# Decay columns first, and four norm weights multiplied into the weights behind them, in a two-layer hybrid trunk on one core

## The chip, the cores and the metric

One Trainium2 chip, one core. The metric is the device time of one execution in microseconds (us). Everything is float32. Products that must be accurate are split by hand into a rounded high part and a rest: three matmuls (high x high, high x rest, rest x high) give one product.

## The reference, cut to what matters

The input x has 256 tokens of 1024 channels. Two layers:

```
def rms_norm(x, w):
    y = x * lax.rsqrt(mean(x * x, -1) + EPS)
    return y * w
hn = rms_norm(h, attn_norm_w[0]);  proj = hn @ w_in            # q, k, v, gate, 16 tail columns
qkv = silu(causal_conv(proj[..., :3072]))
beta = sigmoid(b_logit);  g = -exp(a_log) * softplus(a_logit + dt_bias)   # the tail columns
h = h + (gated delta rule, gated norm) @ w_out
h = h + swiglu(rms_norm(h, ffn_norm_w[0]))                     # d_ff 2816
kv = rms_norm(h, kv_norm_w) @ w_kv                             # shared K and V
q  = rms_norm(h, attn_norm_w[1]) @ w_q;  h = h + attention(q, kv) @ w_o
hn = rms_norm(h, ffn_norm_w[1]);  logits = hn @ router_w
h = h + (top 2 of 8 SwiGLU experts of hn, d_ff 3584)
return rms_norm(h, final_norm_w)
```

## The kernel before, in words

Each engine has its own written-out program, and they meet on semaphores. PE is the matrix engine, DVE the vector engine, ACT the scalar engine, POOL GpSimd, SP the engine that only issues loads. The order on each engine is the order of the code.

**Norms.** A norm k (0 to 5: attention 0, dense, K/V, attention 1, experts, final) is done in two halves of 128 tokens. ACT squares and sums (`square`, L609), POOL makes the reciprocal root (`norm_rstd`, L532 and L533), DVE multiplies by it and by the norm's weight row, which lies broadcast over all partitions (`norm_x`, L945), PE turns the result to channel-major (`turn`, L1478), and ACT and DVE copy it out of the accumulator banks (`turned`, L628 and L955). K/V and queries have the same h and the same reciprocal root, but other weight rows: norms 2 and 3 are two multiplications and two rounds of transposes of the same h.

**Start.** PE turns norm 0, computes the 16 tail columns for half of the tokens (`tail_columns`, L1495, 32 small matmuls in 64 records), transposes the convolution weights (L1504), and goes to `qkv(0)`: first the lower half of the contraction for four column tiles, then the other two groups of tail columns, then the upper half. DVE copies the convolution weights (L961), makes the rest of x (L973) and then the rests of the weights (`q_rest`, L967); ACT makes their high parts (`q_round`, L637); POOL makes every second rest (L540). The tail columns go through ACT exp, DVE (L1000 to L1005), ACT exp and ln, and behind these on ACT stands the first convolution tap (`first_tap`, L676). Each of the 24 column tiles then takes a first tap on ACT, three taps on DVE (`convolve`, L987) and a SiLU on ACT (L662).

**K, V and queries.** After the last down product of the dense MLP, DVE adds to h (L1160), norm 2 follows, and for each token half PE turns x and computes K (L1845) and V (L1851). Then come a swap of halves (L1855), `turn(3)` for the second norm, and the queries (L1869).

**Router and experts.** After attention PE merges heads through w_o (L1928) in 512-column halves, turns norm 4, computes the router's logits (L1968) and counts (L1973 to L1980). DVE takes the two best (`top_two`, L1323 to L1329), makes positions and one-hot matrices (L1341 to L1354), then the rest of the first up weights (`w_rest`, L1169), then the rest of the gathered x (`gathered`, L1383). PE gathers tokens by matmul (L1987) and starts the first expert (`e_proj`, L1508 to L1510). ACT makes the high part of those up weights (`w_round`, L758) after an exp that waits for DVE. Behind `gathered` DVE has the list of items (L1424 to L1444) and then the rest of the next gate weights. The eight experts are blocks of seven steps; a step loads gate, up and down weights of 2 MB each, and SP issues each load as soon as the rest of the slot's former tile is made.

Of the kernel before, what the change touches and what calls it, by code (L numbers as in the profile page):

```python
# [23 lines left out]
P = 128  # L24
# [101 lines left out]
def trunk(nc, ins, consts, cat, out):  # L126
    ctx = ExitStack()
    with ctx:
# [140 lines left out]
        cw = view(sm, 24, CONV * 24)  # L269
        alog = view(sm, 120, 8)  # L270
# [72 lines left out]
        s_oss, s_orstd = sem("s_oss"), sem("s_orstd")  # L343
# [28 lines left out]
        NATIVE = {0: 0, 2: 1, 3: 2, 4: 3}  # L372
# [28 lines left out]
        def _(sp):  # L401
# [57 lines left out]
            for t in range(NT):  # L459
                sp.wait_ge(s_xn, 4 * 4 + 2 * t + 2)  # L460
                sp.dma_start(xn_rows[t * P:(t + 1) * P, :], xn[:, t, :]).then_inc(s_rows, 16)
# [42 lines left out]
            for t in range(NT):  # L504
                for q in range(2):
                    sp.wait_ge(s_xn, 4 * 5 + 2 * t + q + 1)
# [6 lines left out]
        def _(pool):  # L513
# [5 lines left out]
            pool.dma_start(relb[0:BUCKETS, :], ins["rel_bias"]).then_inc(s_relb, 16)  # L519

# [72 lines left out]
        def _(act):  # L593
            link = Chain(act, ach)
            names = [ins["attn_norm_w"][0:1, :], ins["ffn_norm_w"][0:1, :], None,
                     ins["attn_norm_w"][1:2, :], ins["ffn_norm_w"][1:2, :], None]
            names[2] = ins["kv_norm_w"].rearrange("(a n) -> a n", a=1)
            names[5] = ins["final_norm_w"].rearrange("(a n) -> a n", a=1)

            def row_load(k):  # L600
                if k >= 2:
                    act.wait_ge(s_xn, 4 * (k - 2) + 4)
# [14 lines left out]
            def turned(k, groups=range(4)):  # L617
                if k not in NATIVE:
                    for g in groups:
                        t, q = divmod(g, 2)  # L620
                        act.wait_ge(s_tp, 4 * k + g + 1)
# [4 lines left out]
                for g in (g for g in groups if g % 2 == 0):  # L626
                    act.wait_ge(s_tp, 4 * k + g + 1)
# [54 lines left out]
            act.wait_ge(s_small, 16 * 4)  # L682
# [8 lines left out]
            act.activation(nx, nx, ACT.Ln, bias=K("one")).then_inc(s_soft, 1)  # L691
            act.wait_ge(s_cw, 1)
# [77 lines left out]
            row_load(2)  # L770
            row_load(3)
# [50 lines left out]
            for t in range(NT):  # L822
                squares(2, s_h, 4, [t])
                turned(2, [2 * t])
# [11 lines left out]
            turned(3)  # L836
            row_load(4)
            row_load(5)
# [96 lines left out]
        def _(dve):  # L935
            link = Chain(dve, vch)

            def norm_x(k, t):
                if t == 0:
                    dve.wait_ge(s_row[k % 2], 16 * (k // 2 + 1))  # L940
                r = rstd_of(k)
                dve.wait_ge(s_rstd, 2 * r + t + 1)
                for q in range(2):
# [8 lines left out]
            def turned(k, tiles=range(NT)):  # L952
                for g in (2 * t + 1 for t in tiles):
                    dve.wait_ge(s_tp, 4 * k + g + 1)
# [5 lines left out]
            dve.wait_ge(s_cwt, 1)  # L960
# [191 lines left out]
            for n in range(2, NC):  # L1152
                gate_out(n)
# [981 lines left out]
```

## Time and profile before

| | us |
|---|---|
| median of 3 runs | 1515.43 (1514.69 to 1516.58) |
| the profiled execution, its own time | 1515.32 |
| its span, first to last instruction | 1513.5 |
| PE busy | 1472.8 (97% of the span) |
| DVE busy | 1121.9 (74%) |
| ACT busy | 895.3 (59%) |

A busy share says little here by itself: the profile is read by stage. Times in the trace count from the span's start. A row with x64 joins that many records; a matmul's duration overlaps that of the next, so the pace is read from starts or from a group's whole length.

### The profile page before, as it was taken

The numbers are of one execution on the slowest core, as the hardware profiler recorded it, in microseconds if no ns is written. First come the engines' busy times: TensorE is split into PE (matmuls) and PEld (weight loads), VectorE is DVE, ScalarE is ACT, GpSimd is POOL, SyncE is SP. The second block draws the span as 40 slices with busy tenths as digits, with TensorE's granted clock in tenths as the row PEclk, the third lists the DMA queues.
The fourth block names the chain that finished last, engine by engine and source line by source line (L and its number), as shares of the span: only waits on it lengthen the run. The fifth ranks groups of instructions, "written<-read, shape, count | busy, mean of one in ns | idle before, by whom it ended". The sixth has DMA issues, their size and how long they took to land.

```text
span 1513.5 us, 22634 instructions
## 1 busy us (share of the span) xinstructions
PE 1472.8 (97%) x8983; PEld 1233.5 (81%) x8983; DVE 1121.9 (74%) x1057; ACT 895.3 (59%) x851; POOL 96.7 (6%) x65
## 2 busy tenths in 40 slices
PE   6999999999989989999999999999999999999998
PEld 6998958999977577888888888888888888888886
DVE  4766355455434388899888898888888998888796
ACT  4540234434324356777777777677776777777674
POOL 4330010000000000001000000000000000000000
PEclk9999999999999989999999999999999999999999
DMA  7541127555543169999999999999999999999993
GB/s 257 183 152 57 43 72 223 188 170 191 206 182 112 59 244 368 394 386 381 395 376 363 388 375 371 389 377 367 379 373 363 397 393 371 393 377 366 380 393 120
DMA packets 194334, 437.97 MB, mean 289 GB/s; under 512 B 5280, under 2 KB 28096, under 8 KB 194160
## 3 DMA queue, kind: packets, MB, share of 16 engines
q1 hardware_dynamic: 189248, 423.64, 76.0%
q0 software_dynamic: 2736, 9.24, 2.4%
q10 hardware_dynamic: 2304, 4.43, 0.8%
q8 instruction: 35, 0.57, 0.2%
q14 instruction: 11, 0.09, 0.0%
HBM read 429.41 MB, written 7.88 MB: 289 GB/s over the span
## 4 chain that ended last, share of the span: by engine, by line
PE 86%; DVE 7%; ACT 4%; DMA 2%; issue 1%; POOL 1%; DVEq 0%; SPq 0%; ACTq 0%; POOLq 0%
PE bank L1508 23%; PE bank L1510 23%; PE bank L1509 23%; PE bank L1869 2%; PE bank L1928 2%; PE bank L1737 2%; DVE ws L987 2%; PE bank L2043 2%; PE bank L1547 1%; DVE weights_lo L1169 1%; ACT qkv_hi L637 1%; DMA weights<-in_moe_w_down 1%; DMA weights<-in_moe_w_up 1%; PE bank L1652 1%; PE bank L1635 1%
## 5 line engine op out<-in xcount | busy, mean ns | idle before, releaser
L1169 DVE TENSOR_TENSOR weights_lo<-weights,weights_hi 128x2048 fp32r<-128x2048 f32 (+1 forms) x396 | 823.4, 2121 | 142.2 <-ACT weights_hi L758 140.4
L758 ACT ACTIVATE weights_hi<-weights 128x2048 fp32r<-128x2048 f32 (+1 forms) x396 | 685.5, 1782 | 258.8 <-DMA weights<-in_moe_w_up 92.4
L1508 PE MATMUL bank<-weights_hi,expert_x_hi 128*128 128x512 f32 x896 | 354.9, 396 | 1.4 <-DVE expert_x_lo L1383 1.1
L1510 PE MATMUL bank<-weights_hi,expert_x_lo 128*128 128x512 f32 x896 | 349.4, 390 | 0.0
L1509 PE MATMUL bank<-weights_lo,expert_x_hi 128*128 128x512 f32 x896 | 349.2, 390 | 0.0
L1508 PE MATMUL bank<-weights_hi,hidden_hi 128*128 128x512 f32 x520 | 204.4, 393 | 1.5 <-DVE hidden_lo L1207 1.5
L1509 PE MATMUL bank<-weights_lo,hidden_hi 128*128 128x512 f32 x520 | 202.6, 390 | 0.0
L1510 PE MATMUL bank<-weights_hi,hidden_lo 128*128 128x512 f32 x520 | 202.5, 389 | 0.0
L1510 PEld LDWEIGHTS bank<-weights_hi,expert_x_lo 128*128 128x128 f32 x896 | 168.3, 188 | 36.4
L1508 PEld LDWEIGHTS bank<-weights_hi,expert_x_hi 128*128 128x128 f32 x896 | 168.2, 188 | 35.4 <-DVE expert_x_lo L1383 1.2
L1509 PEld LDWEIGHTS bank<-weights_lo,expert_x_hi 128*128 128x128 f32 x896 | 168.4, 188 | 33.4
L1508 PEld LDWEIGHTS bank<-weights_hi,hidden_hi 128*128 128x128 f32 x520 | 97.7, 188 | 22.2 <-DVE weights_lo L1169 2.3
L1510 PEld LDWEIGHTS bank<-weights_hi,hidden_lo 128*128 128x128 f32 x520 | 97.6, 188 | 20.6
L1509 PEld LDWEIGHTS bank<-weights_lo,hidden_hi 128*128 128x128 f32 x520 | 97.7, 188 | 19.4
L1508 PE MATMUL bank<-x_hi,weights_hi 128*128 128x256 f32 x320 | 90.9, 284 | 1.2 <-issue 1.2
L1510 PE MATMUL bank<-x_hi,weights_lo 128*128 128x256 f32 x320 | 90.5, 283 | 0.0
L1509 PE MATMUL bank<-x_lo,weights_hi 128*128 128x256 f32 x320 | 90.5, 283 | 0.0
L777 ACT ACTIVATE ws<-bank 128x512 f32<-128x512 f32 x67 | 39.6, 592 | 82.0 <-PE bank L1510 81.7
L1508 PEld LDWEIGHTS bank<-x_hi,weights_hi 128*128 128x128 f32 x320 | 61.4, 192 | 1.8 <-issue 1.4
L1509 PEld LDWEIGHTS bank<-x_lo,weights_hi 128*128 128x128 f32 x320 | 61.4, 192 | 0.4
L1510 PEld LDWEIGHTS bank<-x_hi,weights_lo 128*128 128x128 f32 x320 | 61.4, 192 | 0.0
L1508 PE MATMUL bank<-qkv_x_hi,qkv_hi 128*128 128x256 f32 x192 | 56.1, 292 | 4.8 <-DVE qkv_x_lo L973 3.7
(312 smaller groups left out, 1498.9 us busy)
## 6 DMA issues: line engine op xcount, KB each, us to landing
weights<-in_moe_w_down SPq DMA_DIRECT2D x56, 2048.0 KB, 9.8
weights<-in_moe_w_up SPq DMA_DIRECT2D x56, 2048.0 KB, 9.7
weights<-in_moe_w_gate SPq DMA_DIRECT2D x55, 2048.0 KB, 9.5
weights<-in_a_w_in SPq DMA_DIRECT2D x7, 2048.0 KB, 8.9
weights<-in_ffn_w_up SPq DMA_DIRECT2D x11, 1024.0 KB, 5.3
weights<-in_ffn_w_gate SPq DMA_DIRECT2D x11, 1024.0 KB, 5.4
weights<-in_ffn_w_down SPq DMA_DIRECT2D x11, 1024.0 KB, 5.0
weights<-in_a_w_out SPq DMA_DIRECT2D x2, 2048.0 KB, 8.1
```

The costliest lines, as they stand in the source:

```text
L637: act.activation(qhi[(c + 1) % 2][:, w_], slot[c % 3][:, w_], ACT.Copy).then_inc(q_hi, 1)
L758: act.activation(hi[:, j * n:(j + 1) * n], slot[k][:, j * n:(j + 1) * n], ACT.Copy).then_inc(w_hi[k], 1)
L777: act.activation(act_h, bank[0][:, :], ACT.Silu).then_inc(m.act, 1)
L987: i_ = dve.scalar_tensor_tensor(out=dst[:, sh:T], in0=src[:, 0:T - sh], scalar=cw[:, w:w + 1], in1=dst[:, sh:T], op0=ALU.mult, op1=ALU.add)
L1169: dve.tensor_tensor(to[:, c], slot[k][:, c], hi[:, c].bitcast(F32), ALU.subtract).then_inc(w_lo[k], 1)
L1508: pe.matmul(dst, ah, bh, start=start, stop=False, skip_group_check=True)
L1509: pe.matmul(dst, ah, bl, start=False, stop=False, skip_group_check=True)
L1510: return pe.matmul(dst, al, bh, start=False, stop=stop, skip_group_check=True)
L1737: m = pe.matmul(bank[banks[q]][:, :], xt[:, kt, t * P:(t + 1) * P], g8[slots[q]][:, kt, :], start=kt == 0, stop=kt == KT - 1)
L1869: m = pe.matmul(bank[3 + g % 2][:, j * T:(j + 1) * T], g8[k][:, kt, c], xt[:, kt, :], start=kt == 0, stop=kt == KT - 1)
L1928: m = pe.matmul(bank[2 * t + q][:, :], oT[:, kt, t * P:(t + 1) * P], g8[q][:, kt, :], start=first and kt == kts[0], stop=last and kt == kt ...
L2043: m = pe.transpose(bank[2][:, j * P:(j + 1) * P], hid[:, j * P:(j + 1) * P], ident)
```

## The change

It does four things. All large buffers keep their addresses: the new small columns lie in gaps.

1. At the start, all four groups of tail columns are computed before `qkv(0)`; the transposes of the convolution weights now also turn three norm-weight vectors (24 more rows, loaded by three small DMAs on POOL's queue). ACT does the exp and ln of the tail ahead of the high parts of the second weight tile; DVE makes the rest of x first and copies the convolution weights after the first weight rest.
2. K/V and queries: DVE multiplies h by the reciprocal root only. ACT multiplies w_kv, and both halves of w_q, in place by the weight column of their norm (`fold`: eight instructions of 128x512 each). Norm 3 with its multiplications, transposes and copies is gone, and so are two row loads. The transposes of the second token half move between K and V of the first.
3. Router: DVE multiplies the router's matrix by the norm weight ahead of time. PE turns h itself instead of norm 4; DVE scales the logits by the reciprocal root. Norm 4's own multiplication, which the gather and the rows in memory still need, comes after.
4. The last merge is cut in two with the first logits between; the first expert's first product waits for each half of the gathered x by itself.

```diff
 ACT, start
             act.wait_ge(s_small, 16 * 7)
             act.activation(alog, alog, ACT.Exp).then_inc(s_soft, 1)
-            for j in range(2):
-                q_round(1, j)
             act.wait_ge(s_tail, 1)
...
             act.activation(nx, nx, ACT.Ln, bias=K("one")).then_inc(s_soft, 1)
+            for j in range(2):
+                q_round(1, j)
             act.wait_ge(s_cw, 1)
 ACT, dense MLP's first norm
-            row_load(2)
-            row_load(3)
+            row_load(4)
+            row_load(5)
 ACT, after the last hidden tile
-            for t in range(NT):
-                squares(2, s_h, 4, [t])
-                turned(2, [2 * t])
+            def fold(i):
+                act.wait_ge(loaded[i], 16 * (PRE_A[i] + 1))
+                for kt in range(KT):
+                    a = act.activation(g8[i][:, kt, :], g8[i][:, kt, :], ACT.Copy, scale=wcol[min(i, 1)][:, kt:kt + 1])
+                a.then_inc(s_fold, 1)
+
+            act.wait_ge(s_cw, 1)
+            fold(0)
+            squares(2, s_h, 4, [0])
+            turned(2, [0])
+            squares(2, s_h, 4, [1])
+            fold(1)
+            turned(2, [2])
+            fold(2)
             act.wait_ge(s_kmm, 1)
...
-            turned(3)
-            row_load(4)
-            row_load(5)
 DVE
+                if k == 2:
+                    for q in range(2):
+                        c = slice(q * 512, (q + 1) * 512)
+                        dve.tensor_scalar(xn[:, t, c], h[:, t, c], rs[:, r, t:t + 1], None, ALU.mult).then_inc(s_xn, 1)
+                    return
...
-            dve.wait_ge(s_cwt, 1)
-            dve.tensor_copy(cw, bank[7][:, 0:96]).then_inc(s_cw, 1)
-            dve.wait_ge(s_cw, 1)
...
             q_rest(0, 1)
-            q_rest(1, 0)
+            dve.wait_ge(s_cwt, 1)
+            for i in range(3):
+                dve.tensor_copy(wcol[i], bank[7][:, 96 + KT * i:96 + KT * i + KT])
+            dve.tensor_copy(cw, bank[7][:, 0:96]).then_inc(s_cw, 1)
+            dve.wait_ge(s_cw, 1)
             def convolve(n):
-                if n % 4 == 0 and 0 < n < 20:
+                if n % 4 == 0 and n < 20:
                     q_rest(n // 4 + 1, 0)
...
+            dve.wait_ge(s_router, 16)
+            dve.tensor_tensor(router[:, :, :], router[:, :, :], wide(wcol[2], E), ALU.mult).then_inc(s_cw, 1)
...
-            dve.wait_ge(s_tp, 12)
-            norm_xn(3)
...
-            turned(3)
 DVE, top_two and its caller
-                link(dve.tensor_copy(logit[:, t, :], bank[4][:, t * 8:t * 8 + 8]))
+                dve.wait_ge(s_rstd, 2 * rstd_of(4) + t + 1)
+                link(dve.tensor_scalar(logit[:, t, :], bank[4][:, t * 8:t * 8 + 8], rs[:, rstd_of(4), t:t + 1], None,
+                                       ALU.mult))
...
-            for t in range(NT):
-                add_h(t, s_aw, 0, (0, 1, 2, 3), 8)
-                norm_x(4, t)
-                if t:
-                    top_two(0)
-                turned(4, [t])
+            add_h(0, s_aw, 0, (0, 1, 2, 3), 8)
+            turned(4, [0])
+            norm_x(4, 0)
+            add_half(1, 0, s_aw, 0, (0, 1, 2, 3))
+            top_two(0)
+            add_half(1, 1, s_aw, 0, (0, 1, 2, 3))
+            turned(4, [1])
             top_two(1)
+            norm_x(4, 1)
 PE
             ready(0)
+            tail_columns(2)
+            tail_columns(3).then_inc(s_tail, 1)
             pe.wait_ge(s_cwin, 16)
-            pe.transpose(bank[7][:, 0:96], convrow[0:96, :], ident[0:96, 0:96]).then_inc(s_cwt, 1)
+            pe.wait_ge(s_small, 16 * 7)
+            pe.transpose(bank[7][:, 0:120], convrow[0:120, :], ident[0:120, 0:120]).then_inc(s_cwt, 1)
...
-                        if half == 0:
-                            tail_columns(2)
-                            tail_columns(3).then_inc(s_tail, 1)
...
+            turn(2, [0])
             for t in range(NT):
-                turn(2, [t])
...
-                pe.wait_ge(loaded[0], 16 * (PRE_A[0] + 1))
+                pe.wait_ge(s_fold, 1)
...
+                else:
+                    turn(2, [1])
...
-            turn(3)
-            ready(3)
...
             turn(4, [0])
-            merge(1, range(8), [1])
-            pe.wait_ge(s_router, 16)
+            merge(1, range(4), [1])
+            pe.wait_ge(s_cw, 2)
             for t in range(NT):
                 if t:
+                    merge(1, range(4, 8), [1])
                     turn(4, [1])
...
             def first_gather():
+                pe.wait_ge(s_xn, 4 * 3 + 4)
...
-            pe.wait_ge(m_Xl, 2)
-            e_proj(0, 0, m_g)
+            e_proj(0, 0, m_g, rows=m_Xl)
```

## Rows read from the trace of the kernel before

**Rows 1.** The page, part 4: the chain that ended last, by engine.
```profile
PE 86%; DVE 7%; ACT 4%; DMA 2%; issue 1%; POOL 1%; DVEq 0%; SPq 0%; ACTq 0%; POOLq 0%
```
**Rows 2.** Windows, expert stage: length, busy of PE, PEld, DVE, ACT, POOL; clock, DMA.
```profile
1090.00:1190.00 100.00, 100.00 (x459) 82.80 (x459) 88.67 (x57) 73.23 (x51) 2.79 (x1) 1.00 1.02 374
```
**Rows 3.** Timeline of the start: start, length, engine, work, idle before and its releaser.
```profile
13.67 3.59 PE L1495 MATMUL bank<-ws,xt 128*64 128x8 f32 x64
14.45 4.55 POOL L540 TENSOR_TENSOR qkv_lo<-weights,qkv_hi 128x2048 fp32r<-128x2048 f32 x1 [3.99 <-ACT qkv_hi L650]
...
17.65 0.26 DVE L961 COPY sm<-bank 128x96 f32<-128x96 f32 x1 [3.18 <-PE bank L1504]
17.94 3.27 DVE L973 TENSOR_TENSOR qkv_x_lo<-xt,qkv_x_hi 128x1024 fp32r<-128x1024 f32 x2
...
21.14 2.28 DVE L967 TENSOR_TENSOR qkv_lo<-weights,qkv_hi 128x2048 fp32r<-128x2048 f32 x1
21.27 0.58 PE L1508 MATMUL bank<-qkv_x_hi,qkv_hi 128*128 128x256 f32 x1 [3.66 <-DVE qkv_x_lo L973]
...
23.95 3.73 ACT L637 ACTIVATE qkv_hi<-weights 128x2048 fp32r<-128x2048 f32 x2 [5.30 <-DMA weights<-in_a_w_in]
...
28.81 2.04 PE L1495 MATMUL bank<-ws,xt 128*64 128x8 f32 x64
...
31.52 1.14 DVE L1002 SCALAR_TENSOR_TENSOR sm<-sm 128x16 f32<-128x16 f32 x1
...
34.44 0.46 ACT L676 ACTIVATE ws<-bank,sm 128x256 f32<-128x256 f32 x1
```
**Rows 4.** The two instructions of line L973: shortest, median, longest in ns.
```profile
L973 DVE TENSOR_TENSOR qkv_x_lo<-xt,qkv_x_hi x2: 1214/1676/2137, 17.9 to 20.0; 128x1024 fp32r<-128x1024 f32 x2
```
**Rows 5.** Windows of PE alone, at the start: length, busy, matmuls, clock, DMA.
```profile
33.00:35.00 2.00, 2.00 (x19) 1.00 0.00 0
```
**Rows 6.** Timeline of the K, V and query stage.
```profile
416.43 0.63 ACT L609 ACTIVATE ws<-h 128x512 f32<-128x512 f32 x1 [7.50 <-DVE h L1160]
...
418.96 1.41 DVE L945 SCALAR_TENSOR_TENSOR xn<-h,sm,norm_row 128x512 f32<-128x512 f32 x2 [1.97 <-POOL sm L533]
...
421.60 0.69 DVE L955 COPY xt<-bank 128x512 f32<-128x512 f32 x1
...
422.40 3.81 PE L1845 MATMUL bank<-xt,weights 128*128 128x128 f32 x32 [1.31 <-issue]
...
431.52 3.81 PE L1845 MATMUL bank<-xt,weights 128*128 128x128 f32 x32 [0.98 <-DVE xt L955]
...
439.48 1.04 PE L1478 MATMUL bank<-cst,xn 128*128 128x128 f32 x8
...
443.39 14.05 PE L1869 MATMUL bank<-xt,weights 128*128 128x256 f32 x64 [0.83 <-ACT xt L628]
```
**Rows 7.** Loads issued at 399.98 and 400.49: size, and us from issue to landing.
```profile
weights<-in_w_kv SPq DMA_DIRECT2D x1, 2048.0 KB, 10.5
weights<-in_b_w_q SPq DMA_DIRECT2D x1, 2048.0 KB, 15.4
```
**Rows 8.** Timeline from the router's logits to the first expert.
```profile
527.89 1.11 PE L1968 MATMUL bank<-router,xt 128*64 128x8 f32 x32
...
534.24 1.88 PE L1968 MATMUL bank<-router,xt 128*64 128x8 f32 x32 [0.88 <-DVE xt L955]
...
539.81 5.79 PE L1987 MATMUL bank<-ws,xn 128*128 128x128 f32 x32 [0.57 <-DVE ws L1345]
...
541.04 4.49 DVE L1169 TENSOR_TENSOR weights_lo<-weights,weights_hi 128x2048 fp32r<-128x2048 f32 x2
...
547.02 0.50 PE L1508 MATMUL bank<-weights_hi,expert_x_hi 128*128 128x512 f32 x1 [1.07 <-DVE expert_x_lo L1383]
...
558.53 0.50 PE L1508 MATMUL bank<-weights_hi,expert_x_hi 128*128 128x512 f32 x1 [0.32 <-DVE weights_lo L1169]
```
**Rows 9.** Load issued at 528: the first expert's first up weights.
```profile
weights<-in_moe_w_up SPq DMA_DIRECT2D x1, 2048.0 KB, 8.4
```

More of the change, by code:

```diff
@@ L269, in trunk @@
         cw = view(sm, 24, CONV * 24)
+        wcol = [view(sm, 372, KT), view(sm, 380, KT), view(ws, 28296, KT)]
         alog = view(sm, 120, 8)
@@ L519, in _ @@
             pool.dma_start(relb[0:BUCKETS, :], ins["rel_bias"]).then_inc(s_relb, 16)
+            for i, w in enumerate((ins["kv_norm_w"], ins["attn_norm_w"][1], ins["ffn_norm_w"][1])):
+                pool.dma_start(convrow[96 + KT * i:96 + KT * i + KT, :],
+                               w.rearrange("(k p) -> k p", p=P)).then_inc(s_small, 16)
             def rstd(dst, src, n, sem_out, inv):
@@ L594, in _ @@
             link = Chain(act, ach)
[L595 to L598, printed above, removed]
+            names = {0: ins["attn_norm_w"][0:1, :], 1: ins["ffn_norm_w"][0:1, :], 4: ins["ffn_norm_w"][1:2, :],
+                     5: ins["final_norm_w"].rearrange("(a n) -> a n", a=1)}
             def row_load(k):
-                if k >= 2:
-                    act.wait_ge(s_xn, 4 * (k - 2) + 4)
+                if k >= 4:
+                    act.wait_ge(s_xn, 4 * (k - 4) + 4)
                 act.dma_start(rows[k % 2][:, :], names[k].to_broadcast([P, D])).then_inc(s_row[k % 2], 16)
@@ L938, in norm_x @@
             def norm_x(k, t):
-                if t == 0:
-                    dve.wait_ge(s_row[k % 2], 16 * (k // 2 + 1))
                 r = rstd_of(k)
+                if t == 0 and k != 2:
+                    dve.wait_ge(s_row[k % 2], 16 * (k // 4 + 1))
                 dve.wait_ge(s_rstd, 2 * r + t + 1)
+                if k == 2:
[3 more added lines that the diff above has]
+                    return
                 for q in range(2):
@@ L995, in _ @@
             dve.wait_ge(s_bexp, 1)
-            dve.wait_ge(s_small, 16 * 4)
+            dve.wait_ge(s_small, 16 * 7)
             tail = view(bank[5], 0, NC, 8)
@@ L1470, in turn @@
                     for q in range(2):
-                        pe.wait_ge(s_xn, 4 * k + 2 * t + q + 1)
+                        if k == 4:
+                            pe.wait_ge(s_h, 8 + 2 * t + q + 1)
+                        else:
+                            pe.wait_ge(s_xn, 4 * k + 2 * t + q + 1)
                         if t and k in NATIVE:
@@ L1477, in turn @@
                             kt = 4 * q + j
-                            m = pe.transpose(bank[6 + q][:, j * P:(j + 1) * P], xn[:, t, kt * P:(kt + 1) * P], ident)
+                            m = pe.transpose(bank[6 + q][:, j * P:(j + 1) * P],
+                                             (h if k == 4 else xn)[:, t, kt * P:(kt + 1) * P], ident)
                         m.then_inc(s_tp, 1)
@@ L1848, in _ @@
                     m.then_inc(s_kmm, 1)
+                else:
+                    turn(2, [1])
                 vm = bank[(5, 2)[t]]
@@ L1862, in query @@
                 if g % 2 == 0:
-                    pe.wait_ge(loaded[k], 16 * (PRE_A[k] + 1))
+                    pe.wait_ge(s_fold, k + 1)
                 if g >= 2:
@@ L2027, in _, with e_proj @@
             eh, el = view(xeh, 0, KT, P), view(xel, 0, KT, P)
-            def e_proj(k, s, done, free=None):
+            def e_proj(k, s, done, free=None, rows=None):
                 if free is not None:
@@ L2033, in e_proj @@
                 for kt in range(KT):
+                    if kt % 4 == 0 and rows is not None:
+                        pe.wait_ge(rows, kt // 4 + 1)
                     if kt % 4 == 0:
```

24 lines of the change are left out of this document (13 added, 11 removed).

## The prediction

> **What bounds the kernel now.** I read the page first. The chain that ended last is matrix work for 86% of the span, DVE for 7% and ACT for 4% [rows 1], so most of the time lies where this change touches nothing. The windows over the expert stage say the same: PE is busy for the whole 100 us at clock 1.00, and the DMA engines are busy throughout too, at 374 GB/s [rows 2]. Nothing there gets shorter; it can only begin earlier. What the change can move are three places where PE isn't the bound: the start, the K/V and query stage, and the way from the router to the first expert. For each I read the timeline engine by engine and asked which instruction starts last.
>
> *Start.* PE stands still between its first tail columns (end 17.26) and 21.27, when DVE has made the rest of x. The lower half of `qkv(0)` then takes until 28.81, the other tail columns 2.0, and from 34.44 on the first taps run [rows 3]. From here ACT and DVE alternate, tap by tap, for all 24 column tiles, and PE waits for them, so the stage is a queue that starts at the first tap: whatever brings that tap forward brings all 24 forward. The tap isn't late because of PE; it stands on ACT behind exp and ln of the tail, and these behind DVE's L1002, which ends at 32.66.
>
> *K, V, queries.* From 422.40 PE works almost without a gap, but a part of it is the second turn of the same h: transposes from 439.48, and queries only at 443.39 [rows 6].
>
> *Router.* PE waits again and again from 529.0, the end of the first logits. Its first expert product at 547.02 is released by DVE's rest of x, behind which DVE's item list runs; the next gate product at 558.53 again waits for DVE [rows 8].
>
> **The change, part one: the start.** The second two groups of tail columns follow the first directly, 17.26 + 3.6 (the same 64 records as at 13.67) = 20.9; the transposes take about 0.4 (the copy behind them starts at 17.65), so PE is free at 21.2 to 21.3. DVE could begin the rest of x earlier now, since the copy is no longer ahead. But the first of the two instructions took 2137 ns and the second 1214 [rows 4]: the first began at 17.94, and POOL's subtraction ran until 19.00 [rows 3]. The 0.92 us more are nearly the 1.06 of overlap, so I let DVE stand still behind POOL here. Started at 15.9 it would be released at 19.0 all the same and be done at 21.3. So `qkv(0)` starts at 21.3 as before. Its lower half still takes 7.5, to 28.8, but the upper half follows at once. Its first tile is twelve matmuls, at 19 in 2.00 us [rows 5] 1.3, at the mean pace of the lower half (48 in 7.5) 1.9: ready at 30.1 to 30.7.
>
> The other input of the tap is ACT. DVE ends the first weight rest at 23.4, copies four small pieces (0.26 for the large one, so 0.3 to 1.0 together), and adds the bias (the whole way from the end of the tail columns, 30.85, to L1002 was 0.7, of which a part was ACT's). L1002 itself took 1.14 for 16 columns, which I can't price: 0.2 if it also stood behind POOL, 1.14 if not; I take 0.3, as POOL has nothing to do then. That gives 24.6 (upper bound 26.2). From L1002's end to the tap were 1.8, and the two high parts of the second tile, which now stand in between, cost 3.73 [rows 3]: 30.1. The first tap starts at 30.4 instead of 34.44: **4.0 us less**, between 2.6 and 4.3. What was hidden before and isn't now: those 3.7 us of ACT; they lie beside PE's lower half, and only if the small chain is late do they show. POOL's next rest starts after them, ends at about 35, and is wanted by PE at 35.8. Three more DMAs on POOL's queue, before its first arithmetic, land while everything still waits for x. What is queued behind PE's new wait for them is `qkv(0)`, which has until 21.2.
>
> **Part two: K, V and queries.** The folds are 24 instructions of 128x512 on ACT. The nearest row is the squaring, 0.63 each [rows 6], so 5.0 per fold. Fold 0 stands ahead of the squares, but ACT was idle for 7.5 us before 416.43. The K/V weights land at 400.0 + 10.5 = 410.5 [rows 7], the fold ends at 415.5, the squares start at 416.43 as before: nothing, with 0.9 to spare. Fold 1 (weights there at 415.9) starts after the second squares at about 422 and ends at 427, fold 2 at 432. The copy of x that waits behind fold 1 isn't wanted before the first V is done (about 430); the copies of K wait behind fold 2 until about 434. The last weights are issued at about 410.5, and even with the longer landing, 15.4, they are there before fold 2. So the folds cost nothing; without that cover they would cost 15.
>
> The normalisation has one operand less. Its row is 1.41 for two halves, with a weight row [rows 6]; the trace has no wide multiplication by a column alone. Bounds: 0.75 each as now, and the 0.28 of a quarter-size one as a floor. I take 0.5, so the copy at 421.60 and K behind it come 0.5 earlier, at 421.9. The Trainium skill (VectorE: DVE Perf Modes, the perf-mode tier table) has 1227 ns for such an operation on 2048 float32 elements in SBUF against 2293 with two tensors; by that ratio each half would be an estimated 0.40 and the gain 0.7. No row here shows it.
>
> PE's work from the first K to the second turn was 422.40 to 439.48, 17.1. The 0.98 of waiting for a copy goes, because K of the other half is now behind V: 16.1. Then 421.9 + 16.1 = 438.0, and the queries follow at 438.1 instead of 443.39: **5.2 us less** (4.8 to 5.7). The four multiplications, 16 transposes and four copies of norm 3 are all in that difference. Two row loads less and two issued elsewhere are beside PE's work.
>
> **Part three: the router.** The first logits now stand ahead of the merge's last half, whose end moves from 527.9 to 529.0. After it, the transposes need only one addition (0.7, as the copies) instead of addition, squares, root and multiplication: logits of the second half at 529.0 + 0.7 + 0.5 (four transposes) + 0.1 + 0.7 = 531.0 instead of 534.24, 1.1 us long as the first or 1.9 as the second [rows 8]. `top_two` comes 3.2 to 4.0 earlier. DVE then has the multiplication of norm 4 (1.4) in front of the positions, at least partly beside PE's counts, so the gather starts 1.8 to 4.0 earlier than 539.81. But that isn't the last input. DVE must first make the rest of the up weights, 4.49, and these are loaded when the merge ends: 529.05 + 8.4 = 537.5 [rows 9], 1.1 later than now. The high parts take 1.9 each (half of 3.73), so DVE runs from 539.3 to 543.8, where it ended at 545.5. **1.7 us less** on DVE. PE starts the expert 2.4 earlier, since it needs only half of the rest of x, but at the next gate product it waited for DVE already, so what is kept is DVE's 1.7. Upper bound 2.9 (the weights are no limit), lower 0 (they land as late as the K/V ones, 10.5). In the expert stage each load is issued by a finished rest, so the loads move with it.
>
> **The sum.** 4.0 + 5.2 + 1.7 = 10.9. The profiled execution has 1515.3 (its span 1513.5 and 1.8 around it), so 1504.4; it is 0.1 below the median of the runs, so I predict **1504.5**. The bounds of the terms make 7.4 to 12.9, 1502.5 to 1508.
>
> **Rivals.**
> - *The router's way gives nothing, or the start only its 2.6.* For it: the up load is issued later and shares the engines with six stores; ACT's chain at the start has three links that I bounded only. Against: later stores leave it more room. 1506.
> - *More.* The load lands early, the multiplication is fast: 4.1 + 5.6 + 2.9 give 1502.8.
> - *Two of the three don't come,* only the queries' part does, with a little: 1509.
> - *A fold shows.* If the K/V weights land 3 us later, the squares start 2 us late and all behind them: 1506.5.
> - *Slower: the expert stage becomes bound by its loads.* DMA is busy for all of it [rows 2], and a step's 6.3 MB at 374 GB/s take just its 16.8 us. If the new phase between PE and the loads stretched a step by more than 10.9 / 56 = 0.19 us, the gain would be gone; at 0.3 the time is 1521. Against: PE has no gap at all, and SP issues on DVE's progress, which shifts as a whole.
> - *No change at all* would need the three waits to be refilled; I see nothing that could do it.
>
> **How the numbers follow.** Forecast 0.46, more 0.19, less at 1506 (with the fold) 0.24, 1509 0.05, slower 0.04, none 0.02. A measurement here tells 0.2%, 3 us, from no change: faster 0.94, same 0.02, slower 0.04. The range 1500.8 to 1508.3 takes in the forecast and its neighbours on both sides and leaves out the last three.
>
> **What would show it.** Right: first L676 near 30.4 and L1508 still near 21.3; queries starting 9.2 earlier than before, 5.2 of it since the dense stage; the squares at the same distance from the last down product; the gate product after the first expert's two 10.9 earlier; 16.8 us per step. Wrong: ACT's fold row directly before the squares with the squares late; the up weights' high part waiting for a DMA beyond 8.4; PE gaps in the expert stage.

## The result and the profile after

The changed kernel takes **1504.42 us** (median of 5 runs, 1502.97 to 1507.0) beside 1515.43 for the kernel before on the same chip (median of 5, 1514.39 to 1520.91). The ratio is 0.9922, with a 95% interval of 0.9909 to 0.9934. Predicted were 1504.5, in a range of 1500.8 to 1508.3. A second set of 5 runs gave 1503.76 and 0.992 [0.9903, 0.9936]. The profiled execution has a span of 1503.0 us against 1513.5, so 10.5 less.

The page of the changed kernel, parts 1 and 4: busy time with its share of the span, and the chain that ended last.

```profile
PE 1467.2 (98%) x8967; PEld 1229.4 (82%) x8967; DVE 1117.8 (74%) x1055; ACT 907.9 (60%) x873; POOL 100.0 (7%) x68
...
PE 78%; DMA 7%; DVE 7%; ACT 5%; issue 3%; POOL 1%; DVEq 0%; SPq 0%; ACTq 0%
```

ACT has 12.6 us more work in a shorter kernel: the folds are 15 us, and its two copies for norm 3, 0.6 us each, are gone. The chain stays matrix work in the main [rows 1]. DMA's part of it is 7% here and was 2% before, but a second trace of the same changed kernel has 1%, so this share differs from one execution to the next.

**The start.** Timeline of the changed kernel; it answers to [rows 3].

```profile
13.37 4.83 PE L1520 MATMUL bank<-ws,xt 128*64 128x8 f32 x128
...
14.45 4.58 POOL L544 TENSOR_TENSOR qkv_lo<-weights,qkv_hi 128x2048 fp32r<-128x2048 f32 x1 [3.83 <-ACT qkv_hi L652]
...
15.83 5.41 DVE L984 TENSOR_TENSOR qkv_x_lo<-xt,qkv_x_hi 128x1024 fp32r<-128x1024 f32 x2 [1.66 <-ACT qkv_x_hi L657]
...
21.17 2.28 DVE L978 TENSOR_TENSOR qkv_lo<-weights,qkv_hi 128x2048 fp32r<-128x2048 f32 x1
21.30 0.58 PE L1536 MATMUL bank<-qkv_x_hi,qkv_hi 128*128 128x256 f32 x1 [2.71 <-DVE qkv_x_lo L984]
...
24.28 0.17 DVE L1017 SCALAR_TENSOR_TENSOR sm<-sm 128x16 f32<-128x16 f32 x1
...
24.49 0.22 ACT L690 ACTIVATE sm<-sm 128x16 f32<-128x16 f32 x1 [5.77 <-DVE sm L1017]
...
26.23 3.71 ACT L639 ACTIVATE qkv_hi<-weights 128x2048 fp32r<-128x2048 f32 x2
...
30.95 0.47 ACT L678 ACTIVATE ws<-bank,sm 128x256 f32<-128x256 f32 x1 [1.01 <-PE bank L1538]
```

The rest of x (L984 here) starts on DVE 2.1 us earlier, and yet `qkv(0)` begins at 21.30, as before (21.27). The small chain is short: L1017 takes 0.17 us where it took 1.14. ACT is ready for the first tap at 29.94. The tap starts at 30.95, because it waits 1.01 us for PE. Before, it started at 34.44, so the start gives 3.5 us.

**K, V and queries.** Timeline of the changed kernel; it answers to [rows 6].

```profile
407.03 5.02 ACT L827 ACTIVATE weights<-weights,sm 128x512 f32<-128x512 f32 x8 [1.64 <-DMA weights<-in_w_kv]
...
412.16 1.29 DVE L1175 TENSOR_TENSOR h<-h,bank 128x512 f32<-128x512 f32 x2 [4.57 <-PE bank L1538]
...
412.88 0.63 ACT L611 ACTIVATE ws<-h 128x512 f32<-128x512 f32 x1 [0.83 <-DVE h L1175]
...
415.39 0.88 DVE L956 TENSOR_SCALAR xn<-h,sm 128x512 f32<-128x512 f32 x2 [1.94 <-POOL sm L537]
...
418.29 3.81 PE L1870 MATMUL bank<-xt,weights 128*128 128x128 f32 x32 [1.27 <-issue]
418.34 5.00 ACT L827 ACTIVATE weights<-weights,sm 128x512 f32<-128x512 f32 x8
...
423.72 4.99 ACT L827 ACTIVATE weights<-weights,sm 128x512 f32<-128x512 f32 x8
...
434.15 2.10 PE L1894 MATMUL bank<-xt,weights 128*128 128x256 f32 x9
```

The first fold ends at 412.05 (407.03 + 5.02) and the squares start at 412.88, released by DVE's addition to h, not by the fold. The other two folds lie beside K and V. The queries start at 434.15 instead of 443.39. That is 9.24 less, of which 3.55 came with the start (the addition to h at 412.16 instead of 415.71).

**From the router to the first expert.** Timeline of the changed kernel; it answers to [rows 8].

```profile
515.14 1.11 PE L1994 MATMUL bank<-router,xt 128*64 128x8 f32 x32
...
519.91 0.37 SPq L408 DMA_DIRECT2D weights<-in_moe_w_up  x1
...
522.19 1.10 PE L1994 MATMUL bank<-router,xt 128*64 128x8 f32 x32 [0.88 <-DVE xt L970]
...
527.24 5.83 PE L2014 MATMUL bank<-ws,xn 128*128 128x128 f32 x32 [0.76 <-DVE ws L1366]
...
528.67 3.71 ACT L760 ACTIVATE weights_hi<-weights 128x2048 fp32r<-128x2048 f32 x2 [2.06 <-DMA weights<-in_moe_w_up]
530.61 4.49 DVE L1189 TENSOR_TENSOR weights_lo<-weights,weights_hi 128x2048 fp32r<-128x2048 f32 x2 [2.05 <-ACT weights_hi L760]
...
535.76 0.50 PE L1536 MATMUL bank<-weights_hi,expert_x_hi 128*128 128x512 f32 x1 [2.35 <-DVE expert_x_lo L1404]
```

The second logits start 12.05 us earlier and the gather 12.57, but the first expert product only 11.26. The gate product after it, at 547.87, is 10.66 earlier than before and waits 0.92 us for DVE. Between them stands a load: ACT waits 2.06 us for the up weights, DVE 2.05 for ACT, PE 2.35 for DVE.

### The profile page after: what moved, and what is told of

Same layout as the page of the kernel before. It is cut to its first block, busy times and chain, and to the rows that moved or that the text cites. A ratio compares the mean times of both kernels' runs of the same rounds, so it can differ in the third digit from the quotient of the medians.

```text
span 1503.0 us, 22624 instructions
## 1 busy us (share of the span) xinstructions
PE 1467.2 (98%) x8967; PEld 1229.4 (82%) x8967; DVE 1117.8 (74%) x1055; ACT 907.9 (60%) x873; POOL 100.0 (7%) x68
## 4 chain that ended last, share of the span: by engine, by line
PE 78%; DMA 7%; DVE 7%; ACT 5%; issue 3%; POOL 1%; DVEq 0%; SPq 0%; ACTq 0%
PE bank L1536 21%; PE bank L1538 21%; PE bank L1537 21%; DMA weights<-in_moe_w_gate 6%; PE bank L1953 2%; PE bank L1894 2%; PE bank L1762 2%; DVE weights_lo L1189 2%; DVE ws L1002 2%; PE bank L1572 1%; PE bank L2072 1%; ACT weights_hi L760 1%; ACT qkv_hi L639 1%; PE bank L1677 1%; DMA weights<-in_moe_w_up 1%
## 5 line engine op out<-in xcount | busy, mean ns | idle before, releaser
L587 POOL DMA_INDIRECT h_rows<-ws,slot_row x7 | 22.5, 3213 | 574.1 <-DVE ws L1424 490.8
```

Of the source, the lines that this page charges most:

```text
L587: pool.indirect_dma_start(out=h_rows[:, :], out_offset=bass.IndirectOffsetOnAxis(ap=slot_row[1][:, 0:1], axis=0), in_=ye, in_offset=None, ...
```

## The experiments

The traces are compared at three marks: the first tap, the start of the queries, and the first down product of the first expert (at 570.82 before, 560.16 after; from here on most steps take 16.8 us in both, those where the expert changes up to 17.6). All times in us, ratios against the kernel before on the same chip.

| kernel | median (runs) | ratio [95%] | tap | queries | down product | down minus queries |
|---|---|---|---|---|---|---|
| before | 1515.43 | 1 | 34.44 | 443.39 | 570.82 | 127.4 |
| the change | 1504.42 (5) | 0.9922 [0.9909, 0.9934] | 30.95 | 434.15 | 560.16 | 126.0 |
| start only | 1512.30 (11) | 0.9975 [0.9964, 0.9985] | 31.03 | 439.9 | 567.99 | 128.1 |
| all but the start | 1508.14 (6) | 0.9951 [0.9932, 0.9969] | 34.47 | 438.1 | 564.02 | 125.9 |
| all but the router | 1507.67 (5) | 0.9937 [0.9918, 0.9955] | 30.66 | 433.8 | 564.33 | 130.5 |
| folds twice | 1514.04 (10) | 0.9987 [0.9975, 0.9999] | 29.68 | 441.2 | 567.05 | 125.9 |
| logits after the merge | 1502.57 (4) | 0.9904 [0.9889, 0.9919] | 31.26 | 434.5 | 559.13 | 124.7 |
| first rest on DVE | 1505.48 (4) | 0.9920 [0.9905, 0.9935] | 30.61 | 433.9 | 562.57 | 128.7 |
| three moves | 1502.84 (5) | 0.9908 [0.9894, 0.9921] | 29.90 | 433.2 | 557.07 | 123.8 |

### The start alone

Into the kernel before: part 1 of the change, without the three norm-weight vectors.

```diff
+            tail_columns(2)
+            tail_columns(3).then_inc(s_tail, 1)
...
-            for j in range(2):
-                q_round(1, j)
             act.wait_ge(s_tail, 1)
...
+            for j in range(2):
+                q_round(1, j)
```

> The kernel before with the start alone changed (all four groups of tail columns first, exp and ln ahead of the second tile's high parts, rest of x first on DVE); nothing is folded. Theory of separate terms: the first tap starts near 31.0 instead of 34.4 and every later stage keeps its distance to it, so the time is 3.5 us less than before, about 1511.9. Rival, overlap: part of the 3.5 is absorbed by a later wait (w_out's load, the dense stage), and it is under 2 us. If the matrix clock rises at another moment, the tap moves by up to 1.2 us either way.

The tap comes at 31.03, 3.4 earlier, and the queries are 3.5 earlier. By medians it is 3.2 us (1515.52 before in these runs), the ratio 0.9975. So the tap's gain goes through all 24 column tiles undiminished. The down product is 2.8 earlier. Of that stage DVE's rest of the up weights still begins 3.5 earlier (537.56 instead of 541.04), the first expert product only 2.8 (544.19 instead of 547.02); between them the gather takes 6.46 us instead of 5.79, and the second half of DVE's rest of x waits 0.81 for ACT's high part of it.

### All but the start

The change, with the start's order as before.

> The changed kernel with the start as before (only the three weight columns are still turned and copied there). Separate terms: first tap at 34.4 or up to 0.5 later for the three copies, queries 5.7 us earlier than before, first expert's second gate product 7.0 earlier, time about 1508.4. Rival: if the start and the rest overlap, this kernel is as fast as the changed one, 1504 to 1505.

The first tap is where it was (34.47), the queries come 5.2 earlier and the down product 6.8, where 5.7 and, at the gate product before it, 7.0 were expected. The missing 0.5 lies between the first tap and the addition to h, which comes at 416.16, 0.45 later than before; from that addition to the queries the gain is the full 5.7. From the queries to the down product it takes 125.9 us, as in the change. The median is 1508.14, 7.4 less than before.

### All but the router

The change, with norm 4 multiplied ahead of its transposes again, the router's matrix as loaded, and the last merge whole.

```diff
-            merge(1, range(4), [1])
-            pe.wait_ge(s_cw, 2)
+            merge(1, range(8), [1])
+            pe.wait_ge(s_router, 16)
...
-            e_proj(0, 0, m_g, rows=m_Xl)
+            pe.wait_ge(m_Xl, 2)
+            e_proj(0, 0, m_g)
```

> The changed kernel with the router's part undone: norm 4 with its weight before the transposes, the plain router matrix, the merge in one piece, one wait for both halves of the gathered x. Separate terms: the start of the last merge is 9.3 us earlier than before, the second gate product too (549.2), time about 1505.8, 1.3 us over the changed kernel. Rival one: the router's part is worth its full 2.9 (1507.3). Rival two: it is worth nothing, because the first up weights now land later (1504.4).

The median, 1507.67, is 3.3 above the change, more than the router's 1.4. The trace points to a reason: in the attention stage the granted clock fell to 0.50 from 483.0 to 489.8, which the change's trace doesn't have, and which cost some 3.0 us in other pairs of traces (below). Without these, 130.5 would be 127.5, the figure of the kernel before. The five times fall into two groups, 1504.8 to 1505.0 and 1507.7 to 1508.3, as such a drop in some executions and not in others would make them; only one of the five has a trace. So the router's 1.4 rests on the marks, and the medians alone would allow the 2.9 of the first rival.

### Every fold twice

Each of the three folds is done with a plain copy of the same tile ahead of it: the price of the folds when their cover runs out.

```diff
+                for kt in range(KT):
+                    a = act.activation(g8[i][:, kt, :], g8[i][:, kt, :], ACT.Copy)
+                link(a)
                 for kt in range(KT):
                     a = act.activation(g8[i][:, kt, :], g8[i][:, kt, :], ACT.Copy, scale=wcol[min(i, 1)][:, kt:kt + 1])
```

> The changed kernel with each fold preceded by a plain copy of the same tile onto itself, so that a fold takes ACT 10 us instead of 5; what is computed is the same. If the folds are hidden with little to spare ahead of the squares and behind fold 2, the squares start 4.2 late, the copy of x behind fold 1 another 2.6, the copy of K behind fold 2 another 3.4: about 10 us more than the changed kernel, 1514.6. If there were ample cover (the idle time of ACT in the profile is longer than that): within 1 us of 1504.4. If the folds already lay fully on the path: 15 us more, 1519.

Timeline of this kernel, K/V and query stage.

```profile
406.02 4.28 ACT L827 ACTIVATE weights<-weights 128x512 f32<-128x512 f32 x8 [1.45 <-DMA weights<-in_w_kv]
...
410.33 5.01 ACT L830 ACTIVATE weights<-weights,sm 128x512 f32<-128x512 f32 x8
...
411.34 1.28 DVE L1178 TENSOR_TENSOR h<-h,bank 128x512 f32<-128x512 f32 x2 [4.57 <-PE bank L1541]
...
415.25 0.61 ACT L611 ACTIVATE ws<-h 128x512 f32<-128x512 f32 x1
...
418.28 1.09 PE L1505 MATMUL bank<-cst,xn 128*128 128x128 f32 x8 [2.96 <-DVE xn L959]
...
420.64 6.70 PE L1873 MATMUL bank<-xt,weights 128*128 128x128 f32 x32 [1.27 <-issue]
...
440.19 1.12 PE L1885 MATMUL bank<-ws,cst 128*128 128x512 f32 x2 [1.50 <-ACT ws L842]
...
441.15 2.11 PE L1897 MATMUL bank<-xt,weights 128*128 128x256 f32 x9
```

Of 12.8 us of added copies, 7.8 show between the addition to h and the queries (29.8 us instead of 22.0). Three places make it up. The first fold now ends at 415.3, after the addition, so the squares and all behind them are 3.2 late. PE stood still for 2.96 us ahead of the transposes, and then the granted clock fell, to 0.50 in the windows from 420 to 426: the same 32 matmuls take 2.9 more. The copies of K, which stand behind the last fold, hold up the swap by 1.5. So in this trace a fold that is 3 us late costs about 6, with the clock drop that follows the wait. The expectation was 1514.6 and the median is 1514.04, but not by the expected terms: the squares are 3.2 late and not 4.2, the copy of x behind fold 1 shows no wait of PE's, the copy of K 1.5 and not 3.4, and the clock, which had no term, 2.9. The trace is also of the fastest of the ten executions, 1510.3. Its queries are 7.0 us later than the change's, its down product 6.9, where the medians differ by 9.6; what fills the rest in the slower executions isn't shown.

### The logits after the whole merge

PE does the last merge in one piece, and the first logits after it; the second half's logits go to another bank, and DVE takes both halves' two best one after the other. This moves the load of the up weights, which is issued when the merge's last instruction has freed its slot, ahead of 1.1 us of logits.

```diff
-            merge(1, range(4), [1])
+            merge(1, range(8), [1])
             pe.wait_ge(s_cw, 2)
...
                 if t:
-                    merge(1, range(4, 8), [1])
                     turn(4, [1])
```

> The changed kernel with the last merge in one piece again and the first logits behind it (the second half's logits go to another bank), top_two(0) directly ahead of top_two(1). Theory: the router's way is bound by the first up weights, which are loaded when the merge ends; here it ends 1.1 us earlier relative to the merge's start, so the load, ACT's high parts and DVE's rest of these weights all come 1.1 earlier, and the expert's products with them: about 1.1 less than the changed kernel. The logits cost nothing, because they lie beside DVE's addition. Rival: DVE's chain from the logits to the one-hot matrices is the bound; top_two(0) now stands in it, and the time is the same or up to 1 us more. In the trace: ACT's wait for the load of moe_w_up stays in the first case and vanishes in the second.

Timeline of this kernel.

```profile
518.98 0.37 SPq L408 DMA_DIRECT2D weights<-in_moe_w_up  x1
...
527.63 3.71 ACT L760 ACTIVATE weights_hi<-weights 128x2048 fp32r<-128x2048 f32 x2 [1.15 <-DMA weights<-in_moe_w_up]
...
534.73 0.50 PE L1536 MATMUL bank<-weights_hi,expert_x_hi 128*128 128x512 f32 x1 [1.18 <-DVE expert_x_lo L1404]
```

The load is issued 0.93 earlier, ACT's high part, PE's first expert product and the down product all come 1.03 to 1.04 earlier, though this execution's queries were 0.31 later than the change's. Counted from the queries it is 1.3. The logits themselves come later, and that costs nothing: the load is what the expert waits for.

### The first rest on DVE instead of POOL

```diff
-            for c in range(6):
-                pool.wait_ge(q_hi, 2 * c + 2 if c else 1)
+            for c in range(1, 6):
+                pool.wait_ge(q_hi, 2 * c + 2)
...
-            q_rest(0, 1)
+            for half in range(2):
+                q_rest(0, half)
```

> The changed kernel with the very first weight rest made by DVE, behind the rest of x, instead of by POOL beside it. Theory: DVE's rest of x took 5.4 us for two instructions because it stands still while POOL's subtraction of two tensors runs. Without POOL both take 1.2 each, from 15.8 to 18.2, the two weight rests follow until 22.7, qkv(0) can start at 20.5 instead of 21.3, and the small chain is 0.7 earlier: first tap 0.7 to 0.8 earlier than in the changed kernel (30.95), give or take the moment at which the matrix clock rises. Rival: the long duration is the instruction's own (its operands are strided); then the rest of x ends at 21.2 again, the first weight rest at 23.4, and the first tap is 2 us later.

The two instructions of the rest of x, shortest, median and longest in ns, in the change and in this kernel; the first answers to [rows 4].

```profile
L984 DVE TENSOR_TENSOR qkv_x_lo<-xt,qkv_x_hi x2: 1212/2744/4275, 15.8 to 20.0; 128x1024 fp32r<-128x1024 f32 x2
```

```profile
L984 DVE TENSOR_TENSOR qkv_x_lo<-xt,qkv_x_hi x2: 1218/1222/1225, 16.0 to 17.2; 128x1024 fp32r<-128x1024 f32 x2
```

With POOL idle both take 1.22 us, so the length isn't the instruction's own, as the rival had it. With POOL's subtraction beside it the first takes 4.28, and it ends at 20.1, 1.07 us after POOL's end at 19.03: of its 1.22 us it got at most 0.15 done until POOL was through. The Trainium skill (SBUF — State Buffer, two separate sides) describes this as an exclusive lock on a port pair shared by DVE and GpSimd, held for a whole instruction. By that rule the trace agrees. Still the tap is only 0.34 earlier (30.61) and not 0.7 to 0.8, since it waits for PE, 1.30 us here. And PE was no earlier: `qkv(0)` starts at 21.36 and not at the expected 20.5. The rest of x is done at 18.4, but PE is busy with the tail columns until 21.3:

```profile
14.29 7.00 PE L1521 MATMUL bank<-ws,xt 128*64 128x8 f32 x128 [0.66 <-DMA ws<-in_a_w_in]
...
21.36 0.56 PE L1537 MATMUL bank<-qkv_x_hi,qkv_hi 128*128 128x256 f32 x1
```

The same 128 records took 4.83 us in the change; why is told with the prediction's start below. The down product came later than in the change, with 128.7 us behind the queries: this trace too has the clock at 0.78 and 0.53 in the two windows from 480 to 490, and says nothing of the edit there.

### Three moves together

The last two edits, and ten instructions of DVE's item list (count, comparison, running sum) moved from behind `gathered` to the time in which DVE waits for the up weights.

> Both edits before together, and the first ten instructions of DVE's item list (counts, blocks over 128, ranks; 2.0 us) moved ahead of the rest of the first up weights, where DVE stood idle for 2.05 us waiting for the load. Theory: the second gate product waits for DVE's list and rest (0.92 us of PE idle), and the idle time before it can hold a part of the list: 0.7 to 0.8 at the start, 1.1 from the load, 0.9 at the second gate product, together 2.5 to 2.9 less than the changed kernel, 1501.7. Rival: only the part that isn't limited by the load's landing comes, 1 us or less.

Its trace is the shortest of all, a span of 1498.3, with the down product 3.1 earlier than in the change, of which 0.9 is there at the queries. The gate product waits for nothing any more. But its median, 1502.84, is 1.6 below that of the change, with intervals that overlap. So it was timed again, with the change and the merge variant on one chip.

> The change once more, unaltered, to give the two variants a partner that shares their chip and their runs. If the scatter seen so far is what single executions do in the expert stage and in the clock's first rise, the median is 1504.4 within 1.5, the ratio 0.992 within 0.001.

> The change with the whole last merge ahead of the first logits, once more. Theory (the first expert's up weights are issued when the last merge ends, so a shorter way to that point brings the expert forward): 1.1 to 1.3 us less than the unaltered change, about 1503.2. Rival (the 1.9 us seen between medians was scatter, and the load's landing moves with something else): the same as the unaltered change within 0.5.

> The change with three moves, once more. Theory: its trace had the expert's third mark 3.1 us earlier than the change, 2.1 of it behind the start, so 2 to 3 us less than the unaltered change beside it, 1501.5 to 1502.5. Rival (the profiled execution was a lucky one, and only the merge's order counts): as the variant with the merge alone, within 0.5.

| kernel, again | median (runs) | ratio [95%] | queries | down product |
|---|---|---|---|---|
| the change | 1503.76 (5) | 0.992 [0.9903, 0.9936] | 434.25 | 560.05 |
| logits after the merge | 1504.66 (5) | 0.9916 [0.9898, 0.9934] | 434.02 | 561.77 |
| three moves | 1504.16 (6) | 0.9918 [0.99, 0.9936] | 433.12 | 559.98 |

Neither variant is faster than the change by anything that these times can tell, so both expectations of a gain in the median fell; the change itself came within the 1.5 us expected of it. The traces say why a single execution moves by 3 us. Here are windows (length, busy and count of PE, PEld, DVE, ACT, POOL; clock; DMA) of the merge variant's first trace, and of its second, the same kernel.

```profile
480.00:485.00 5.00, 3.84 (x48) 2.51 (x44) 4.46 (x24) 2.36 (x8) 0.00 (x0) 1.00 0.01 3
485.00:490.00 5.00, 5.00 (x30) 2.60 (x29) 2.17 (x7) 3.39 (x17) 0.00 (x0) 1.00 0.00 0
```

```profile
480.00:485.00 5.00, 4.08 (x40) 2.76 (x40) 4.55 (x24) 2.26 (x7) 0.00 (x0) 0.82 0.01 3
485.00:490.00 5.00, 5.00 (x28) 2.82 (x27) 2.48 (x7) 3.11 (x17) 0.00 (x0) 0.50 0.00 0
```

In the second the clock falls to 0.50, its lower level of 1.2 GHz, between 480 and 485 and is back at 490. From the queries to the down product it takes 127.7 us instead of 124.7: 3.1 more. The three-move kernel has 126.9 with the drop and 123.8 without. The change itself has 126.0 and 125.8 in its two traces. So, counted from the queries and without the drop, the merge's order gives 1.1 to 1.3 us and the three moves 2.0 to 2.2, and one drop hides either.

## Why the prediction was right

**The start: mechanism right, 4.0 predicted, 3.5 found.** Right were the order (DVE held by POOL and done at 21.2, `qkv(0)` at 21.30), ACT's chain (ready at 29.94 where 30.1 was predicted), and the small L1017 at 0.17. The tail columns ended at 18.2 (13.37 + 4.83) and not at 20.9, which didn't count, since PE waits for DVE anyway. The reason is the clock. Here are windows (length, busy PE with count; clock; DMA, GB/s) in the change, and in the second trace of the merge variant, whose start is the same:

```profile
14.00:16.00 2.00, 2.00 (x76) 1.00 1.05 387
16.00:18.00 2.00, 2.00 (x44) 0.51 1.06 389
```

```profile
14.00:16.00 2.00, 2.00 (x40) 1.00 1.05 388
16.00:18.00 2.00, 2.00 (x42) 1.00 1.04 384
```

Where the records run at 76 in 2 us, the clock was at its higher level; at 40 to 44 it was at the lower one. (The second trace's clock column can't be used here: its record has no entry before 25.8, and the column shows 1.00 where there is none.) With the lower level throughout, the tail columns take 7.0 us, as twice the 3.6 of the kernel before would have it, and end at 20.9. That is the case in five of the nine other traces with the new start. The mis-sized step is the upper half on PE: the first tile of the upper half was put at 30.1 to 30.7, and the tap waited for PE until 30.95. The lower half's pace was taken from before, 48 matmuls in 7.5 us; in the change the matmuls stood 0.21 us apart until 26.2, in the kernel before until about 25.1, and 0.12 after; the record has the clock's rise from 0.50 to 1.00 at 26.27 in the one and its first entry, 1.00, at 25.12 in the other. In the trace with doubled folds, whose start is the same, this pace ended at 23.9, with the clock's rise, and the tap came at 29.68 with only 0.19 us of waiting for PE. So ACT, ready at 29.94 in the change, would have allowed 4.5, and when the clock rises decides how much of it comes.

**K, V and queries: 5.2 predicted, 5.7 found.** The folds follow one another every 0.62 (predicted 0.63) and cost nothing. The squares wait for h, as predicted, though the margin was 0.83 instead of 0.9. The multiplication by a column alone was sized right: its records are 0.48 to 0.49 long, taken were 0.5, and the pair takes 0.88 instead of 1.41. By the table of the Trainium skill (VectorE: DVE Perf Modes, the perf-mode tier table) the estimate was 0.40; the measured length lies above it. K starts 6.13 after the addition to h where it took 6.69, a gain of 0.56. The prediction's own terms give 438.1 for the queries, 5.3 less and not 5.2. The mis-sized term, and the rest of the difference, is the "16.1": from the first K to the queries it is 15.86 us, and I had 16.1 and 0.1 behind it. The turn between K and V costs 0.87 from its start to V's, where turn and waiting took 2.02 before (429.50 to 431.52), so 1.15 went and not 0.98; and the 0.1 behind the swap isn't there.

**Router: 1.7 predicted, 1.4 found.** The chain went as predicted. Logits and gather came earlier by 2.8 to 3.3 beyond the stages ahead (a part of it by the clock, which was 0.50 at the second logits before and 1.00 in the change: 1.88 and 1.10 us), and the load was what DVE's rest waited for. Counted from the queries it was issued 1.16 later than before (predicted 1.1), and it took 8.7 instead of 8.4: the mis-sized step is the landing. DVE's rest of these weights is therefore done only 1.2 earlier than before, counted from the queries, and not 1.7. Another 0.2 came by something that the prediction had no term for. Before, the second half of DVE's rest of x waited for ACT's high part of it (done at 546.24, the half begun at 546.27); in the change the two follow one another at once. Two lines of before, and one of the change:

```profile
545.45 1.52 DVE L1383 TENSOR_TENSOR expert_x_lo<-bank,expert_x_hi 128x512 fp32r<-128x512 f32 x2
545.64 0.60 ACT L890 ACTIVATE expert_x_hi<-bank 128x512 fp32r<-128x512 f32 x1 [1.41 <-PE bank L1987]
```

```profile
535.02 1.28 DVE L1404 TENSOR_TENSOR expert_x_lo<-bank,expert_x_hi 128x512 fp32r<-128x512 f32 x2
```

The landing moves from one execution to the next: it was 8.5 in the second trace of the change, and there the router's gain is 1.6. The merge variant tells this reading from a rival, that the logits decide: it makes the logits later and the load earlier, and the expert came earlier. The kernel without the router's part has 127.5 us behind the queries when the clock drop is taken off, and the kernel before 127.4. All traces with the router's part, and with the merge as in the change, have 125.8 to 126.0 where the clock didn't drop. The upper bound, 2.9, was not reached for the reason given.

**The sum.** At the down product 3.55 + 5.69 + 1.42 = 10.66 us are gained, at the end of the span 10.5. From there to the end it is 942.7 us before and 942.8 in the change, so next to nothing was given back. Two of the three part-kernels fit by medians: start alone 3.2, all but the start 7.4, together 10.6 against 11.0 and 11.7 for the change. The third, all but the router, fits by the marks only. Two of my errors, 0.5 too much at the start and 0.5 too little at the queries, cancelled. That is luck: the median hit the forecast closer than its terms deserve.

**The rivals.** *Two of three don't come* and *no change* are refuted by the part-kernels. *A fold shows* didn't happen, since the K/V weights landed in time; in the trace with doubled folds 3 us of lateness cost about 6, as the clock fell behind the wait. *Slower, bound by the loads*: most steps take 16.81 or 16.82 us in both. Behind the first down product PE waits once to three times, 0.2 to 1.4 us, in eight of the twelve traces, and in four it never does. Ahead of the three longest of these waits ACT had waited for loads; the link wasn't tested. The stage from the down product to the end took 941.2 to 943.8 us over all kernels, 942.7 in the kernel before, 942.8 and 941.5 in the two traces of the change. That is scatter of single executions and no new pace. If the mechanism is at work, its price is at most 0 to 2.6 us per execution: 1.5 before, and 1.6 and 0.3 in the change's two traces, with the shortest stage taken as free of it.

**Left open.** Why the clock drops near 484 in four of the eight traces in which the queries begin near 434, and in none of the other four, wasn't found; the two traces of one kernel differ in it, so the program alone doesn't decide it. They come from two chips, but each of these chips gave traces with the drop and traces without. In the four the fall comes 48.9 to 49.2 us behind the queries' start. At the start of the kernel these four have the first tail columns at the lower level. Of the other four, three had them at the higher one from about 13 to 16, and the fourth, the three moves, had not. So what the clock did earlier may have a part in it; no run tests that. Why the clock rises at the start only at 23.9 to 26.7 wasn't found either.

## What to carry to other kernels

Look for the same large operand normalised twice: a weight vector along the contraction can go into the weights, on an engine and at a time that have cover, and the second normalisation, transposes and copies vanish with it. When a step is moved forward, follow the load behind it too: here everything around the router came some 3 us earlier, and 1.4 was kept, since the next weights were issued 1.2 us later within the stage. And where variants differ by 1 or 2 us, compare traces from mark to mark before believing medians, for a single clock drop costs 3.

## What the runs showed of the hardware beyond the expected

- **The doubled wait.** A PE wait of 2.96 us ahead of eight transposes was followed by a clock of 0.50 for about 6 us, and 32 matmuls that take 3.81 us in the change needed 6.70. In this one trace the wait cost as much again.
- **A drop without a cause in the program.** The same kernel, once on each of two chips: once 1.00 throughout the attention stage, once 0.82 and 0.50 in two windows. It costs 3.1 us.
- **A clock column that shows 1.00 where nothing was recorded.** At the start, matmuls of 256 columns stand 0.21 us apart in every trace, and 0.12 later. In the change the windows show the clock's level with it. In the kernel with the first rest on DVE they show 1.00 at the slow pace (length, busy PE with count, clock, DMA; the change first):

```profile
22.00:24.00 2.00, 2.00 (x11) 0.50 1.02 402
26.00:28.00 2.00, 2.00 (x18) 0.93 1.05 385
```

```profile
22.00:24.00 2.00, 2.00 (x11) 1.00 0.93 367
24.00:26.00 2.00, 2.00 (x14) 1.00 1.04 389
```

The second trace's record has its first entry at 25.44, and there the pace changes. So it is in all twelve: the change of pace and the entry of 1.00 (from 23.9 to 26.7) lie within 0.1 us of each other, and in seven of them that entry is the first. Ahead of a record's first entry the level is read from the count of matmuls in a window.

- **Beside a subtraction of POOL's, DVE's stands nearly still.** A DVE subtraction of 1.22 us, started 1.4 us into POOL's, ended 1.07 after POOL's end. Small instructions suffer more. POOL's next subtraction in the kernel before:

```profile
27.76 4.87 POOL L540 TENSOR_TENSOR qkv_lo<-weights,qkv_hi 128x2048 fp32r<-128x2048 f32 x1 [8.76 <-ACT qkv_hi L637]
```

It ended at 32.63, and DVE's L1002, begun at 31.52, ended at 32.66 and took 1.14 us; in the change nothing of POOL's is beside it, and it takes 0.17. That is the price I couldn't read in [rows 3].
